# Norm factors spread by the factor column times the identity, after the first scores; first conv sums on GpSimd in 512 columns

## The reference, cut to what matters

```python
def rmsnorm(x, g):
    xf = x.astype(jnp.float32)
    y = xf * lax.rsqrt(jnp.mean(xf * xf, axis=-1, keepdims=True) + EPS)
    return (y * g.astype(jnp.float32)).astype(x.dtype)

    for i in range(DEPTH):
        h = rmsnorm(x, g_mix[i])
        proj = h @ w_in[i]
        ...
        mem_kv = rmsnorm(mem, g_mem[i]) @ w_mem_kv[i]
        mem_out = memory_cross_attention(q_mem, mem_kv, g_q[i], g_k[i])
        x = x + jnp.concatenate([mixed, mem_out], axis=-1) @ w_out[i]
        h = rmsnorm(x, g_ffn[i])
        gate, up = jnp.split(h @ w_ffn_in[i], 2, axis=-1)
        x = x + (jax.nn.silu(gate) * up) @ w_ffn_out[i]
```

## Time and profile before

| what | us |
|---|---|
| median of 3 runs | 2652.38 (2651.53 to 2652.42) |
| profiled execution, first to last instruction (its span) | 2646.9 |
| PE busy | 2562.6 (97%) |
| DVE busy | 1784.0 (67%) |
| ACT busy | 1204.7 (46%) |
| GpSimd busy | 719.9 (27%) |

### The profile page before, as it was taken

How to read it: one execution, slowest core, us unless ns; L and a number is a source line. 1 busy time by engine, 2 the same in 40 slices (tenths; PEclk the granted TensorE clock), 3 DMA queues, 4 the chain that set the end, 5 groups by cost and what they waited for, 6 DMA issues and landing times.

```text
span 2646.9 us, 34791 instructions
## 1 busy us (share of the span) xinstructions
PE 2562.6 (97%) x12320; PEld 2130.7 (80%) x12320; DVE 1784.0 (67%) x2247; ACT 1204.7 (46%) x2027; POOL 719.9 (27%) x523
## 2 busy tenths in 40 slices
PE   8899999999999999999999999998899999999999
PEld 8688887888888887887878888886788888887887
DVE  6566666167756577775677777777648665758667
ACT  6463333144434443335666666665424443444332
POOL 2502220102323222233033333333120322222322
PEclk9899999999999999999999999999999999999999
DMA  6412225213433456534111111112321342437634
GB/s 208 152 40 72 78 90 191 80 63 116 146 116 119 151 177 246 217 147 159 49 37 33 33 32 32 32 32 107 125 101 53 139 161 77 152 133 273 236 145 157
DMA packets 85923, 311.39 MB, mean 118 GB/s; under 512 B 10417, under 2 KB 10417, under 8 KB 73137
## 3 DMA queue, kind: packets, MB, share of 16 engines
q1 hardware_dynamic: 74304, 261.17, 28.0%
q0 software_dynamic: 11216, 42.47, 4.5%
q10 hardware_dynamic: 288, 6.29, 0.6%
HBM read 220.24 MB, written 89.65 MB: 117 GB/s over the span
## 4 chain that ended last, share of the span: by engine, by line
PE 79%; DVE 7%; issue 7%; ACT 4%; POOL 1%; DMA 1%; SPq 0%; ACTq 0%; DVEq 0%; POOLq 0%
PE ps L2334 25%; PE ps L2336 24%; PE ps L2335 24%; PE ps L2646 1%; POOL sig L968 1%; DVE aT_lo L1955 1%; PE ps L2662 1%; DVE tile_lo L2203 1%; DVE w_lo L1584 1%; DVE keep L1913 1%; ACT keep L1313 1%; PE ps L2663 1%; PE ps L2595 1%; ACT sq L1325 1%; PE ps L2596 1%
## 5 line engine op out<-in xcount | busy, mean ns | idle before, releaser
L2334 PE MATMUL ps<-tile_hi,g_hi 128*128 128x512 f32 x1680 | 661.3, 394 | 7.7 <-DVE tile_lo L2203 5.2
L2336 PE MATMUL ps<-tile_hi,g_lo 128*128 128x512 f32 x1680 | 658.3, 392 | 0.0
L2335 PE MATMUL ps<-tile_lo,g_hi 128*128 128x512 f32 x1680 | 654.7, 390 | 0.0
L2334 PE MATMUL ps<-xg_hi,w_hi 128*128 128x512 f32 x1024 | 412.6, 403 | 4.5 <-DVE xg_lo L1783 3.3
L2336 PE MATMUL ps<-xg_hi,w_lo 128*128 128x512 f32 x1024 | 402.6, 393 | 0.0
L2335 PE MATMUL ps<-xg_lo,w_hi 128*128 128x512 f32 x1024 | 402.1, 393 | 0.0
L2334 PEld LDWEIGHTS ps<-tile_hi,g_hi 128*128 128x128 f32 x1680 | 316.2, 188 | 76.1 <-issue 5.5
L2336 PEld LDWEIGHTS ps<-tile_hi,g_lo 128*128 128x128 f32 x1680 | 316.0, 188 | 71.5
L2335 PEld LDWEIGHTS ps<-tile_lo,g_hi 128*128 128x128 f32 x1680 | 316.3, 188 | 69.0
L1482 ACT ACTIVATE g_hi<-quads 128x512 fp32r<-128x512 f32 x310 | 194.9, 629 | 359.0 <-PE ps L2336 328.8
L2132 DVE TENSOR_TENSOR g_lo<-quads,g_hi 128x512 fp32r<-128x512 f32 x310 | 281.4, 908 | 107.1 <-ACT g_hi L1482 103.1
(11 more groups left out here) (277 smaller groups left out, 4338.4 us busy)
## 6 DMA issues: line engine op xcount, KB each, us to landing
quads<-wpack SPq DMA_DIRECT2D x62, 1024.0 KB, 5.9
raw<-wpack SPq DMA_DIRECT2D x88, 512.0 KB, 3.3
d_split<-x SPq DMA_DIRECT2D x116, 256.0 KB, 6.3
tile_lo<-d_tile SPq DMA_DIRECT2D x30, 512.0 KB, 7.5
d_tile<-R SPq DMA_DIRECT2D x46, 256.0 KB, 6.4
d_tile<-x SPq DMA_DIRECT2D x46, 256.0 KB, 6.1
cquads<-wpack SPq DMA_DIRECT2D x10, 1024.0 KB, 4.8
tile_hi<-d_split SPq DMA_DIRECT2D x10, 1024.0 KB, 8.5
```

The source lines that it names most:

```text
L2334: pe.matmul(out, whi, mhi, start=start, stop=False, skip_group_check=chained)
L2335: pe.matmul(out, whi, mlo, start=False, stop=False, skip_group_check=chained)
L2336: return pe.matmul(out, wlo, mhi, start=False, stop=stop, skip_group_check=chained)
```

## The change

- `diag` and `kdiag`, their DVE instructions and their semaphores go. `spread_factors` is eight float32 matmuls: the stationary operand is one column of recip, broadcast to 128 x 128, the moving one is the identity. R is copied without a factor, and the constant in g_qk is divided by 128. A float32 matmul is two instructions in the trace, so that 4 become 16 in each of the six spreads.
- In stage B of both layers PE does `scores(0)` and `scores(1)` first, then the spread, into banks 2 and 3, after a wait for rqv_ready (bank 3 read) and recip_ready (bank 5 read). `scores(0)` no longer waits for `r_ready`; batch 1 does. The statistic of head 1 and its root on ACT and DVE move from ahead of the loop into batches 1 (PE) and 2 (ACT, DVE). ACT copies R after the first exponentials.
- GpSimd's four sums of x become 16 of 128 x 512, and start when head 0's rq is ready; ACT waits for 16 steps where it waited for 4.

```diff
@@ GpSimd, layer 0
                     pool.wait_ge(acc_added, 2 * KB)
-                    a11, a21, a12, a22 = c_sum[0], c_sum[1], c_sum[3], c_sum[6]
-                    part(0, a11, a11, a21, ALU.subtract)
-                    part(1, a21, a21, a22, ALU.add)
-                    part(2, a22, a22, a11, ALU.subtract)
-                    part(3, a12, a12, a22, ALU.subtract)
+                    pool.wait_ge(rq_ready, 1)
+                    for k in range(4):
+                        a11, a21, a12, a22 = (c_sum[q][:, k, :] for q in (0, 1, 3, 6))
+                        part(4 * k, a11, a11, a21, ALU.subtract)
+                        part(4 * k + 1, a21, a21, a22, ALU.add)
+                        part(4 * k + 2, a22, a22, a11, ALU.subtract)
+                        part(4 * k + 3, a12, a12, a22, ALU.subtract)
@@ ScalarE
-                act.activation(R[:], banks(4), ACT.Copy, scale=float(P)).then_inc(r_ready, 1)
+                act.activation(R[:], banks(4 if nu % 2 else 2), ACT.Copy).then_inc(r_ready, 1)
...
                 query_root(0)
-                query_root(1)
-                norm_spread(2 * i)
                 prep(u0 + 4)
                 exps(0)
+                norm_spread(2 * i)
...
-                    if n in (6, 10):
+                    if n in (2, 6, 10):
                         query_root(n // 4 + 1)
...
-                    act.wait_ge(csum_step, 4)
+                    act.wait_ge(csum_step, 16)
@@ VectorE
             def norm(nu):
 
                 reciprocals((root_ready, nu + 1), LAYERS + nu + 1)
-                diagonal(diag, diag_ready)
...
                 reciprocals((kroot_ready, i + 1), i + 1)
-                diagonal(kdiag, kdiag_ready)
...
                 query_root(0)
-                query_root(1)
                 prep(u0 + 4)
...
-                    if n in (6, 10):
+                    if n in (2, 6, 10):
                         query_root(n // 4 + 1)
@@ TensorE
-            def spread_factors(src, b, signal):
-
-                for h in range(2):
-                    last = pe.matmul(ps[:, b + h, :], mean_head[:], src[:, 4 * h:4 * h + 4, :].rearrange("p a c -> p (a c)"),
-                                     start=True, stop=True)
+            def spread_factors(b, signal):
+
+                for j in range(KB):
+                    last = pe.matmul(ps[:, b + j // 4, j % 4 * P:(j % 4 + 1) * P], recip[:, j:j + 1].to_broadcast([P, P]),
+                                     ident[:], start=True, stop=True)
                 last.then_inc(signal, 1)
...
                     if n == 0:
                         pe.wait_ge(kv_loaded, 64 * (i + 1))
-                        pe.wait_ge(r_ready, 2 * i + 1)
...
                 quarter_unit(2, 0)
-                pe.wait_ge(diag_ready, 2 * i + 1)
-                spread_factors(diag, 4, spread)
-                qstat(1)
                 scores(0)
+                pe.wait_ge(recip_ready, LAYERS + 2 * i + 1)
                 scores(1)
+                pe.wait_ge(rqv_ready, MHEADS * i + 1)
+                spread_factors(2, spread)
                 quarter_unit(2, 1)
                 for n in range(BATCHES):
-                    if n in (5, 9):
+                    if n == 1:
+                        pe.wait_ge(r_ready, 2 * i + 1)
+                    if n in (1, 5, 9):
                         qstat(1 + n // 4)
```

More of the change, by code:

```diff
@@ L192, in trunk @@
         squares.append(squares[1])
-        diag = place("diag", [P, KB, P], F32, Z + 60 * K1)
         mem = place("mem", [P, KB, NMEM], F32, Z)
@@ L199, in trunk @@
         ksq = place("ksq", [P, MHEADS * NMEM], F32, Z + 28 * K1)
-        kdiag = place("kdiag", [P, KB, P], F32, Z + 32 * K1)
         ka_hi = place("ka_hi", [P, MHEADS * NMEM], F32R, Z + 40 * K1)
@@ L332, in trunk @@
         recip_ready = sem("recip_ready")
-        diag_ready = sem("diag_ready")
         spread = sem("spread")
@@ L347, in trunk @@
         kroot_ready = sem("kroot_ready")
-        kdiag_ready = sem("kdiag_ready")
         kspread = sem("kspread")
@@ L1594, in reciprocals @@
                 dve.wait_ge(ready[0], ready[1])
-                if done > 1:
-                    dve.wait_ge(recip_ready, done - 1)
                 dve.reciprocal(recip[:], root[:]).then_inc(recip_ready, 1)
-                dve.wait_ge(recip_ready, done)
-            def diagonal(dst, signal):
-                dve.tensor_tensor(dst[:], ident[:].unsqueeze(1).to_broadcast([P, KB, P]),
-                                  recip[:].unsqueeze(2).to_broadcast([P, KB, P]), ALU.mult).then_inc(signal, 1)
             def norm(nu):
                 reciprocals((root_ready, nu + 1), LAYERS + nu + 1)
-                diagonal(diag, diag_ready)
             def scaled(dst, b, h):
@@ L1627, in _ @@
             prep(1)
-            dve.scalar_tensor_tensor(g_qk[:], g_heads[:, 0, :], float(P) ** 0.5, g_heads[:, 1, :],
+            dve.scalar_tensor_tensor(g_qk[:], g_heads[:, 0, :], float(P) ** -0.5, g_heads[:, 1, :],
                                      ALU.mult, ALU.mult).then_inc(gqk_ready, 1)
@@ L2399, in _ @@
                 if i > 0:
-                    pe.wait_ge(kdiag_ready, i)
-                    spread_factors(kdiag, 6, kspread)
+                    pe.wait_ge(recip_ready, i)
+                    spread_factors(6, kspread)
                 if i == 0:
@@ L2500, in _ @@
                     pe.wait_ge(evacuated, v0)
-                    pe.wait_ge(kdiag_ready, LAYERS)
-                    spread_factors(kdiag, 6, kspread)
+                    pe.wait_ge(recip_ready, LAYERS)
+                    spread_factors(6, kspread)
                 unit(u0, 0, lambda h: h, (None, None), first=2 * i, halves=(1,))
@@ L2816, in _ @@
                 unit(u0, 0, lambda h: h, (v0 - 3, v0 - 2), first=nu, halves=(1,), ks=range(2, 5))
-                pe.wait_ge(diag_ready, nu + 1)
-                spread_factors(diag, 4, spread)
+                pe.wait_ge(recip_ready, LAYERS + nu + 1)
+                spread_factors(4, spread)
                 unit(u0, 0, lambda h: h, (v0 - 3, v0 - 2), first=nu, halves=(1,), ks=range(5, KB))
```

## The result

The changed kernel takes 2661.65 us (median of 5 runs, 2660.01 to 2668.44), the kernel before 2651.53 (2650.36 to 2652.42): 10.1 us more, a ratio of 1.0044 [1.0032, 1.0056]. The forecast was 2647.1, with 2650.6 as the upper end. It is slower by twice what a measurement can tell from no change.

The account below looks back on a forecast made before the run. The prediction took PE, 79% of the chain that ended last, as the bound. Memory keys -1.27, layer 0 -5.7, layer 1 +1.3 and SwiGLU +0.4 summed to -5.3: 2647.1 us, range 2643.6 to 2650.6.

Parts of the forecast that it names:

- the gain is given back: Rival: transfers joining the layers are due at their own pace, so PE waits for them later; 2651 us, chance 0.08.
- 2654.6: Rival of loads in series: each spread instruction pays load and stream, 7.5 us on PE's path; chance 0.07.
- Memory keys: Second memory's spread of key factors no longer waits for kdiag: -1.47, +0.20 for its longer form, -1.27 us.
- The new form: Sixteen float32 instructions of 128 columns per spread take 1.92 us, 0.20 more than now (between -0.04 and +1.7).
- Layer 0: First quarter's end to batch 2's scores: PE works back to back, waits for R and exponentials go; -5.7 us.
- GpSimd's sums: Sixteen narrow sums run beside batches 0 to 2 and end at about 135; cost 0, up to +2.5 us.
- one of the prediction's signs of being wrong: The forecast is wrong if PE waits for prob or nbias in batches 0 to 3; no size given.
- the rival of blocked DVE steps: Batches 0 to 2: rq's small steps for head 1 meet GpSimd's pieces, +1 to +3, about 2649.3 us; chance 0.16.
- Layer 1: Before the scores PE waits about 2.7 us for keys and values, with a slow clock behind: +1.3 us.
- The ends given there: Layer 1: +1.3 us with wait and slow clock; -2.3 with the transfer as quick as in layer 0.
- SwiGLU: SwiGLU norms: the diagonal was hidden, so only the two longer spreads count, 2 x 0.20 = +0.4 us.

Follow-up runs that it names:

- 12 idle instructions against 4: Changed kernel with 12 or 4 waits on an already signalled semaphore added at PE's start: 2645.05 us with 12, 2661.64 us with 4.
- 60 against none: Changed kernel with 60 waits on an already signalled semaphore added at PE's start: 2643.14 us; the changed kernel without them: 2661.65 us.
- 60, 32 and 12 idle instructions: Changed kernel with 60, 32 or 12 already signalled waits added at PE's start: 2643.14, 2645.07 and 2645.05 us; kernel before 2651.53 us.
- all five kernels that fetch 82 pieces: Changed kernel with 0 or 4 idle waits at PE's start: 2661.65, 2661.64 us; kernel before with 76, 96 or 122: 2666.97, 2665.97, 2674.33 us.

## Why the prediction was wrong

**The step that failed is a term that isn't in the sum.** "-1.27 - 5.7 + 1.3 + 0.4 = -5.3" runs over the places that the change touches and puts all other code at nothing, without a reason. The change adds 122 PE instructions ahead of a loop, and this shift costs 16.6 us (12 idle instructions against 4), or 18.5 (60 against none), at a place 300 us behind the last of them. The -5.3 became +10.1. The rival "the gain is given back" named transfers (weights, mixed rows) that are due at their own pace, and gave back at most what was gained; no case of mine went above 2654.6, since I had counted instructions only by what each lasts.

The number to see it was in the profile of before: 64 packets on the instruction queue, none between 1524 and 1819, so that the loop was resident, and a body of over 6 pieces. That 122 more instructions fall on the wrong side could not be read from it without the edges. What such a case was worth is known only from the runs: the slow positions begin somewhere from 187 to 202 and end at 255, 54 to 69 of 256. By this estimate a case of about 0.25 at +16 was missing among the rivals.

**Memory keys**, forecast -1.27: the spread starts at 90.21, right behind the unit, instead of 92.00. The mechanism is right; what follows it (80 to 120) moved by -1.8 in this execution and by -1.1 to +0.1 in the others with the new spread, so the size is within the drift. **The new form**, forecast 1.92 for sixteen: 1.95. Right. By the Trainium skill (TensorE: Matmul & The Clock Gate, "Part 3: Packing small matmuls", "The mechanism") loads of all rows would not overlap. The trace speaks against this rule, as the 512-column form did: with load and stream in series the prediction had 3.4. In the slow clock of layer 1 the same sixteen last 3.62.

**Layer 0**, forecast -5.7 and the scores of batch 2 at about 125: -5.2 (-5.2 to -7.0 in the six others with the new order and narrow sums) and 123.83. Right. **GpSimd's sums**, forecast 0 and an end near 135: they end at 138, since some are longer (up to 2.22); nbias takes up to 1.07 and prob 1.79, three times. The cost of about nothing is right, but one of the prediction's signs of being wrong did come: PE waits for prob in batch 3, behind two of head 1's steps to rq that last 0.76 and 1.15 instead of 0.17.

```profile
139.97 0.66 PE L2450 MATMUL ps<-ident,prob 128*128 128x128 f32 x4 [0.37 <-DVE prob L1730]
```

This is the rival of blocked DVE steps, at 0.37 us instead of 1 to 3. What the forecast did not see is how much hangs on them: with the old width the new order loses 8.5 us. It had put rq's blocking down as the cause of a wait and not as the condition for the gain.

**Layer 1**, forecast +1.3: +2.4 in the changed kernel, and -0.6 to +0.7 in six others with the same order and the same wait. The ends given there, -2.3 and +1.3, were too low for the changed kernel by 1.1, while the price for a typical execution was lower than forecast. **SwiGLU**, forecast +0.4: within the drift of single executions, not told.

Taken together without the loop, the forecast of -5.3 stands against -8.2, -6.3, -6.9 (60, 32 and 12 idle instructions against before, by the medians): the right sign and two thirds to five sixths of the size.

## What to carry to other kernels

Count the instructions that a change puts ahead of a long loop, not only what they last: look for the instruction queue in the profile, see whether it falls silent during the loop, and how many pieces of 256 the body touches together with the piece behind it (eight were the limit here). If a change is slower at a place that it doesn't touch, with waits on "issue" at jumps back, shift the code by some tens of idle instructions before you judge the change. And take two obstacles away together before calling either of them worthless: the narrow sums gave 1.4 us alone, the order lost 2.1 alone (neither clear of the intervals), and together they gave 6.3.

## What the hardware showed that I had not expected

- A jump back to code that was pushed out costs a fetch of about 2.7 us (its packet starts at 1535.4, PE's first instruction comes at 1538.1), PE idle for 3.3 to 5.1, then a second stop of 1.9 to 2.5 if the target lies under ten instructions ahead of an edge (none with 34 and 54), and the lower clock behind them (windows of 0.50 in all five kernels that fetch 82 pieces): 5.1 to 10.6 us in all for each jump.
- Eight instructions of nothing at the start of PE's program are worth 16.6 us of 2650.
- GpSimd's sums of 1.3 us beside DVE's steps cost DVE up to 1.1 for each, and PE 0.37 in the changed kernel; those of 4.6 us cost it 3.6 to 4.3 for each, and PE 7.72 in one wait in the new order.
